# Conv features of a hybrid decoder block by seven products per tile pair, attention in a stage of its own

## The reference

```python
proj = jnp.einsum('bsd,de->bse', x, w_in[l])
q, k, v, cb, cc, ch, g_conv, g_attn = jnp.split(proj, SPLIT_POINTS, axis=-1)
# short convolution: three causal taps per channel over u = cc * ch, then times cb
y_conv = short_conv_mixer(cb, cc, ch, conv_w[l])
# blocks of 128 queries against 256 keys; ALiBi bias, mask, and a sink logit in max and denominator
y_attn = sliding_window_attention(q, k, v, attn_sinks[l])
merged = jax.nn.sigmoid(g_conv) * y_conv + jax.nn.sigmoid(g_attn) * y_attn
mix = jnp.einsum('bse,ed->bsd', merged, w_out[l])
x = layer_norm(ALPHA * x + mix, ln1_g[l], ln1_b[l])
hid = jax.nn.silu(x @ w_gate[l]) * (x @ w_up[l])
x = layer_norm(ALPHA * x + hid @ w_down[l], ln2_g[l], ln2_b[l])
```

## Time and profile before

| | before |
|---|---|
| median of three runs | 1379.73 us |
| the profiled execution's own time | 1379.17 us |
| its span, first to last instruction | 1377.3 us |
| TensorE busy | 1366.4 us, 6650 matmuls |
| VectorE busy | 779.7 us |
| ScalarE busy | 484.3 us |
| GpSimd busy | 596.9 us |
| mean granted TensorE clock | 0.999 |

### The profile page before, as it was taken

The page is one execution under the profiler, slowest core; times in us unless marked ns, Lnnn a source line. Parts: engine busy times, 40 slices in busy tenths (PEclk is TensorE's granted clock), DMA queues, the critical chain, the costliest instruction groups (busy, mean ns, idle before and its releaser), DMA issues. The chain is left out here.

```text
span 1377.3 us, 19023 instructions
## 1 busy us (share of the span) xinstructions
PE 1366.4 (99%) x6650; PEld 1200.2 (87%) x6650; DVE 779.7 (57%) x1197; ACT 484.3 (35%) x933; POOL 596.9 (43%) x375
## 2 busy tenths in 40 slices
PE   9999999999999999999999999999999999999997
PEld 8888888888888888888888888888888888888886
DVE  3127564566447653767967944645456454464547
ACT  4434333344243433335245332322323213233143
POOL 2221223212322132124885493754737547475474
PEclk9999999999999999999999999999999999999999
DMA  6211111111111111111430131112211112121113
GB/s 184 62 46 46 41 37 51 40 46 46 46 46 34 42 46 46 46 45 48 136 93 31 46 91 33 62 52 62 69 31 61 53 61 69 31 65 56 55 54 123
DMA packets 128406, 80.22 MB, mean 58 GB/s; under 512 B 8432, under 2 KB 123120, under 8 KB 128368
## 3 DMA queue, kind: packets, MB, share of 16 engines
q1 hardware_dynamic: 128368, 79.73, 19.2%
HBM read 75.53 MB, written 4.19 MB: 58 GB/s over the span
## 5 line engine op out<-in xcount | busy, mean ns | idle before, releaser
L512 POOL TENSOR_TENSOR w_lo<-raw,w_hi 128x1024 fp32r<-128x1024 f32 x54 | 128.4, 2378 | 480.0 <-ACT w_hi L663 471.0
L1448 PE MATMUL ps<-act_hi,w_hi 128*128 128x512 f32 x848 | 322.5, 380 | 0.0
L1449 PE MATMUL ps<-act_lo,w_hi 128*128 128x512 f32 x848 | 321.4, 379 | 0.0
L1450 PE MATMUL ps<-act_hi,w_lo 128*128 128x512 f32 x848 | 321.4, 379 | 0.0
L604 POOL TENSOR_TENSOR w_lo<-raw,w_hi 128x512 fp32r<-128x512 f32 x80 | 110.4, 1381 | 204.0 <-ACT w_hi L886 204.0
L1450 PEld LDWEIGHTS ps<-act_hi,w_lo 128*128 128x128 f32 x848 | 160.2, 189 | 22.8
L1449 PEld LDWEIGHTS ps<-act_lo,w_hi 128*128 128x128 f32 x848 | 160.4, 189 | 21.6
L1448 PEld LDWEIGHTS ps<-act_hi,w_hi 128*128 128x128 f32 x848 | 160.3, 189 | 21.6
L1448 PE MATMUL ps<-hid_hi,wd_hi 128*128 128x512 f32 x320 | 121.5, 380 | 0.1
L1449 PE MATMUL ps<-hid_lo,wd_hi 128*128 128x512 f32 x320 | 121.3, 379 | 0.0
L1450 PE MATMUL ps<-hid_hi,wd_lo 128*128 128x512 f32 x320 | 121.3, 379 | 0.0
(11 more groups left out here) (213 smaller groups left out, 2539.2 us busy)
## 6 DMA issues: line engine op xcount, KB each, us to landing
raw<-in_w_in SPq DMA_DIRECT2D x52, 512.0 KB, 3.8
raw<-in_w_gate SPq DMA_DIRECT2D x40, 256.0 KB, 2.9
raw<-in_w_up SPq DMA_DIRECT2D x40, 256.0 KB, 3.1
raw_d<-in_w_down SPq DMA_DIRECT2D x20, 512.0 KB, 3.2
raw<-in_w_out SPq DMA_DIRECT2D x16, 512.0 KB, 3.7
xs<-in_x SPq DMA_DIRECT2D x8, 512.0 KB, 7.2
out<-rows SPq DMA_DIRECT2D x7, 512.0 KB, 2.6
raw_first<-in_w_down SPq DMA_DIRECT2D x2, 512.0 KB, 3.5
```

Of the source, the lines that this page charges most:

```text
L512: pool.tensor_tensor(w_lo[:, slot], raw[:, slot], fp(w_hi[:, slot]), ALU.subtract).then_inc(w_lo_s, 1)
L1448: pe.matmul(bank, w_h(t), hi, start=(t == 0), stop=False)
L1449: pe.matmul(bank, w_h(t), lo, start=False, stop=False)
L1450: last = pe.matmul(bank, w_l(t), hi, start=False, stop=(t == tiles - 1))
```

## The change

The loop over heads is replaced by two stages written out in line.

- **Conv stage.** Twelve tile pairs, (cc, ch) of all eight conv tiles and (gc, cb) of the four even ones, are computed by seven products each, as in the FFN. Blocks of w_in of 256 KB are loaded to `raw`; GpSimd forms four sums or differences and seven low parts of 128x512 for each pair. The four token sums of x are kept in `x_form`, formed by VectorE, ScalarE and GpSimd in the prologue; x's second half is kept in `res` by an extra copy (`x_kept`), the sum of the parts of the first half is formed by GpSimd (`x_sum_first`). The taps of the convolution are done within `conv_pair`.
- **Attention stage.** 24 tiles stay as units of 24 matmuls: q, ga, and the odd gc and cb of each head, 12 units to four heads' queries in place of 24. Positions of all work are counted in depth steps of three matmuls, eight to a unit: block b has its scores at 12b, the turning at 12b + 14, the values at 12b + 20, and the other engines follow lists sorted by such positions. The first block stands at the end of the four units of the first q tiles. The last head's blocks 5 to 7 run into the output projection, whose first half starts before its second half's operands exist.
- **Sink.** The sink is an extra column of the score tile, so the maximum, the exponent and its sum contain it; the score is kept negated. Four small VectorE operations and one ScalarE operation of a block fall away (`SOFT` 8 to 4).
- **Out-projection.** `x_sum(1, m)` moves from the first half's loop to the second half's, one ahead of each `out_sum`; the second half's low parts (`mix_second`) go to the end of the attention.

The output computed is the same. The core of the diff:

```diff
+CONV_PAIRS = [pair for k in range(NKV) for pair in (("cc", "ch", 2 * k), ("gc", "cb", 2 * k), ("cc", "ch", 2 * k + 1))]
+HEAD_TILES = [(0, "q", 0), (0, "q", 1)]
+for _k in range(NKV):
+    HEAD_TILES += [(_k, "ga", 0), (_k, "ga", 1), (_k, "gc", 1), (_k, "cb", 1)]
+    if _k < NKV - 1:
+        HEAD_TILES += [(_k + 1, "q", 0), (_k + 1, "q", 1)]
+UNITS = [(0, 0), (0, 1), (1, 0), (1, 1)]
...
+def block_at(b, later):
+    return TURN_OF * (b // NB) + 12 * (b % NB) + later
+PE_STEPS = sorted([(block_at(b, 0), "scores", b) for b in BLOCKS] + [(block_at(b, 14), "turn", b) for b in BLOCKS]
+                  + [(block_at(b, 20), "values", b) for b in BLOCKS])
+DVE_STEPS = scheduled(
+    [(unit_end(u) + (0.2 if HEAD_TILES[UNITS[u][0]][1] == "cb" else 0.9), "unit", u) for u in range(len(UNITS))
+     if HEAD_TILES[UNITS[u][0]][1] != "ga"],
+    [(block_at(b, 1), "scores", b) for b in BLOCKS],
+    [(block_at(b, 8.2), "exp", b) for b in BLOCKS],
+    [(block_at(b, 16.2), "turn", b) for b in BLOCKS],
+    [(block_at(b, 22.2), "values", b) for b in BLOCKS],
+    [(-28 if k == 0 else TURN_OF * k - 7.5, "keys", k) for k in range(NKV)],
+    [(-27 if k == 0 else TURN_OF * k - 3.5, "bias", k) for k in range(NKV)],
...
+            for c in range(NCP):
+                for j in range(7):
+                    conv_product(c, j)
+            def scores(b):
+                k, n = b // NB, b % NB
+                if n == 0:
+                    pe.wait_ge(prep_dve, 8 * k + 2)
+                    pe.wait_ge(q_lo_s, 8 * k + (4 if k else 8))
...
+            def values(b):
+                k, n = b // NB, b % NB
+                pe.wait_ge(pt_lo_s, k * NTURN + (turned(n, 1) + 1))
...
+            act.wait_ge(c_pair, CONV_STEPS)
+            for step, n in ACT_STEPS:
...
+            def taps(h):
+                y = res[:, j, half(h)]
+                done(f"gate{h}")
+                dve.tensor_scalar(y, u_pad[:, h * HALF:(h + 1) * HALF], cw[:, j, 0:1], None,
+                                  ALU.mult).then_inc(c_pair, 1)
+                for t in (1, 2):
+                    dve.scalar_tensor_tensor(out=y, in0=u_pad[:, h * HALF + t:(h + 1) * HALF + t],
+                                             scalar=cw[:, j, t:t + 1], in1=y, op0=ALU.mult,
+                                             op1=ALU.add).then_inc(c_pair, 1)
...
-                    dve.tensor_reduce(mx[:], prob[:, :, lo:], AX_X, ALU.max).then_inc(soft_s, 1)
-                    dve.tensor_tensor(mx[:], mx[:], snkc[:], ALU.max).then_inc(soft_s, 1)
+                dve.tensor_reduce(neg_m[:], sc[:, :, lo:], AX_X, ALU.min).then_inc(soft_s, 1)
...
+            for v in range(DT, OUT_TILES):
                 if v != OUT_TILES - 2:
+                    x_sum(1, v - DT)
                     out_sum(v)
+                if v == OUT_TILES - 3:
+                    x_sum(1, DT - 2)
```

More of the change, by code:

```diff
@@ L49 @@
 PRO_TILES = 4
-TILES = [("q", 0), ("q", 1), ("ga", 0), ("ga", 1)] + [(x, j) for j in (0, 1) for x in ("cc", "ch", "gc", "cb")]
 PRO_UNITS = [(0, 0), (1, 0), (0, 1), (1, 1), (2, 0), (2, 1), (3, 0), (3, 1)]
-NT = len(TILES)
-IN_TILES = PRO_TILES + NKV * NT
-OUT_TILES = 2 * DT
-COLS = {"q": COL_Q, "ga": COL_GA, "cc": COL_CC, "ch": COL_CH, "cb": COL_CB, "gc": COL_GC}
[L60 to L74, removed]
@@ new lines, with conv_table, conv_step @@
+CONV_B = {"u2": 1, "u3": 2, "up0": 3, "gate0": 4, "hid0": 5, "up1": 6, "part1": 7, "sum1": 8, "gate1": 9, "hid1": 10}
+def conv_table(c):
+    return CONV_A if CONV_PAIRS[c][0] == "cc" else CONV_B
+def conv_step(c, name):
+    return sum(max(conv_table(b).values()) for b in range(c)) + conv_table(c)[name]
+CONV_STEPS = conv_step(NCP - 1, "taps1")
+HEAD_TILES = [(0, "q", 0), (0, "q", 1)]
[3 more added lines that the diff above has]
+        HEAD_TILES += [(_k + 1, "q", 0), (_k + 1, "q", 1)]
@@ L514, in _, with x_sum_first @@
             pool.wait_ge(w_first_s, 1)
-            for t in range(6):
-                low_part(t + 1, t % 2)
+            def x_sum_first(m):
+                if m == 0:
+                    pool.wait_ge(x_lo_s, 8)
+                pool.tensor_tensor(res[:, m, half(0)], fp(act_hi[:, m, half(0)]), fp(act_lo[:, m, half(0)]),
+                                   ALU.add).then_inc(x_sum0, 1)
+            low_part(1, 0)
+            for m in (0, 4):
+                x_sum_first(m)
+            low_part(2, 1)
@@ L978, in _, with keep_values @@
                                   fp(act_hi[dst]), ALU.subtract).then_inc(x_lo_s, 1)
-            for i in range(4):
+            def keep_values(i):
                 j, h = PRO_UNITS[i]
@@ L989, in mixer_low @@
+            for c in range(NCP):
+                conv_pair(c)
+            dve.wait_ge(c_pair, CONV_STEPS)
             def mixer_low(h, m):
@@ new lines, in turn_probs @@
+            def turn_probs(b):
+                k, n = b // NB, b % NB
+                pe.wait_ge(soft_s, SOFT * b + SOFT)
+                if b:
+                    pe.wait_ge(pt_lo_s, k * NTURN + turned(n, 1 if n == 0 else 0))
+                for kb in range(1 if n == 0 else 0, 2):
+                    for g in range(G):
+                        last = pe.transpose(ps[:, TURN + kb, blk(g)], prob[:, g, blk(kb)], ident[:])
+                    last.then_inc(turn_s, 1)
+            def values(b):
+                k, n = b // NB, b % NB
+                pe.wait_ge(pt_lo_s, k * NTURN + (turned(n, 1) + 1))
+                if n == 0:
+                    pe.wait_ge(prep_dve, 8 * k + 8)
+                if b:
+                    pe.wait_ge(o_s, 3 * (b - 1) + 2)
+                kbs = [1] if n == 0 else [0, 1]
+                for kb in kbs:
+                    for part in (pt_hi, pt_lo):
+                        last = pe.matmul(ps[:, OUT, :], vs[:, n - 1 + kb, :], folded(part[:, kb]),
+                                         start=(kb == kbs[0] and part is pt_hi),
+                                         stop=(kb == 1 and part is pt_lo))
+                last.then_inc(values_s, 1)
```

946 lines of the change are left out of this document (613 added, 333 removed).

## The result

The changed kernel takes 1387.95 us in the median (1386.09 to 1390.26, 4 runs) against 1379.65 (1379.35 to 1380.01, 4 runs) for the kernel before: a ratio of 1.0061, with a 95% interval of 1.0041 to 1.008. It is slower by 0.6%, clear of the noise. The forecast was 1372.0 and the range ended at 1386.

What follows compares the result with a forecast made beforehand. TensorE was taken as the bound, busy 1366.4 of 1377.3 us. 31.1 us saved against 23.8 us of new waits gave 1379.2 - 7.3 = 1371.9, rounded to 1372 us; range 1357 to 1386.

Steps and rivals of the forecast that it cites:

- What is removed: Twelve tile pairs: 144 fewer matmuls at 0.216 us each on TensorE, saving 31.1 us.
- the floor: Time with the full saving and no new TensorE waits: 1379.2 - 31.1 = 1348.1 us.
- Prologue and conv stage: Kernel start and conv products: new TensorE waits of 0.3 us (bounds 0 and 4) and 1 us in all.
- port rival: Conv stage: GpSimd and VectorE sharing the port exceed TensorE's time, 10.4 us in all, 1382 us; chance 0.13.
- Handover and first scores: Wait before the first q unit, 4.9 us; block 0's wait for the q low parts, 2.9 us.
- Interior blocks: Attention blocks not at a head's end: VectorE's work fits on average, 0.5 us of waits for all.
- rival of late low parts in every block: Attention: each of 28 interior blocks late by 0.7 us, costing 19 us, time 1391; chance 0.13.
- Head ends: Last block of a head, before its values: low parts late, 2 us at each of three, 6 in all (bounds 0 and 12).
- The last block: Output projection, first half: last block's low parts late behind mix_second and x_sum, 3.2 us (bounds 0 and 6).
- `mean(1)`: Output projection, second half: three more x_sums delay mean(1) in full, 4.5 us taken (2.1 to 6.5).
- The clock: Low granted clock at the gap before the first q unit: 0.5 us added for the way back (bounds 0 and 3).
- 0.15 on slower: Whole kernel: chance 0.15 that the time comes out over 1382.5 us.

Runs made afterwards that it cites:

- last-block experiment: Changed kernel with the six late mixer low parts moved behind the last block's low part on VectorE: 1385.67 us, 1.0042 of the kernel before.
- experiment on the sums of the second half: Changed kernel with five second-half x_sums moved after the first half and three ahead of out_sum(9): 1382.83 us, 1.0032 of the kernel before.
- all waits taken up: Changed kernel with five reorderings together (first weight parts, head ends, mixer low parts, second-half sums, first scores): 1357.64 us, 0.9845 of the kernel before.
- what was left: The all waits taken up kernel with four mixer low parts behind out_sum(5), last head's mixer steps a block later, second mean two steps later: 1356.01 us.

## Why the prediction failed, step by step

**What is removed: right.** The own time 1386.09 less 29.7 of gaps and 8.5 of clock is 1347.9; the floor was put at 1348.1.

**Prologue and conv stage: right, but for a term that comes and goes.** In the profile of the changed kernel neither has a new gap (0 against 1.3 taken). In three of the ten profiles of kernels with the conv stage there is one of 1.98 us near 85, always at the fourth product of the second pair (`THIRD_DIFF`), waiting for VectorE's first sum `u2`. VectorE of the last-block experiment there:

```profile
80.20 1.68 DVE L1372 TENSOR_TENSOR u_pad<-cu_st,cu 128x512 f32<-128x512 f32 x1
81.92 1.39 DVE L1326 TENSOR_SCALAR res<-u_pad,cw 128x512 f32<-128x512 f32 x1
```

The product into u_pad took 1.68 us and the first tap 1.39, where the changed kernel's profile has 0.92 and 0.49. In the one GpSimd's low parts began at 80.06, just ahead of the product, in the other at 79.37, behind it (78.26 to 79.18). So who comes first decides on 1.7 us of VectorE's time here. These kernels' first units also start up to 1.2 us apart. The port rival was thus wrong in the size (10 us) and right in the place. GpSimd is not full in the conv stage of the changed kernel (fifth of the busy times), and TensorE idles only behind its end:

```profile
78.00:277.00 199.00, 197.89 (x917) 172.90 (x915) 114.35 (x140) 55.98 (x93) 154.51 (x116) 1.00 0.21 59
```

**Handover and first scores: right.** 4.9 taken, 4.95 measured; 2.9 taken, 2.99 measured. Both chains were walked in full from rows 3 to 6, with nothing beside them. **Interior blocks: right** (0.5 taken, none measured but the 0.67 at 641, put down to issue), and so the rival of late low parts in every block was wrong.

**Head ends: right in place and cause, 1.8 us short.** Three of 2.6 us against three of 2. The walk had the low parts at 18.0 us from the scores of the head's last block (376.8 at the first end); there they ended at 396.55, 19.8 us on. Most of the difference is one operation, the gating (L1470): 2.00 us beside a GpSimd weight part of 2.37, where 0.43 is its time alone. The prediction had named this collision and allowed 1.5 us for it.

**The last block: mechanism right, size under half.** Taken at 3.2 us (bounds 0 and 6), measured 7.01. TensorE, VectorE and GpSimd in the changed kernel:

```profile
650.62 1.89 PE L1791 MATMUL ps<-m_hi,w_lo 128*128 128x512 f32 x8
659.35 0.77 PE L1957 MATMUL ps<-pt_hi,vs 128*128 128x512 f32 x1 [6.84 <-DVE pt_lo L1456]
659.91 0.63 PE L1957 MATMUL ps<-pt_lo,vs 128*128 128x512 f32 x1
```

```profile
648.01 3.48 DVE L1381 SCALAR_TENSOR_TENSOR m_lo<-res,m_hi 128x512 fp32r<-128x512 f32 x2
651.40 0.68 DVE L1475 TENSOR_TENSOR res<-act_hi,act_lo 128x512 f32<-128x512 f32 x1
652.19 0.69 DVE L1524 SCALAR_TENSOR_TENSOR res<-res,ps 128x512 f32<-128x512 f32 x1
652.79 5.10 DVE L1381 SCALAR_TENSOR_TENSOR m_lo<-res,m_hi 128x512 fp32r<-128x512 f32 x3
657.81 1.27 DVE L1456 TENSOR_TENSOR pt_lo<-ps,pt_hi 128x512 fp32r<-128x512 f32 x2
```

```profile
647.69 2.64 POOL L739 TENSOR_TENSOR w_lo<-raw,w_hi 128x1024 fp32r<-128x1024 f32 x1 [1.98 <-ACT w_hi L1056]
652.95 1.65 POOL L728 TENSOR_TENSOR acc<-acc,res 128x512 f32<-128x512 f32 x1 [2.62 <-DVE res L1524]
654.56 2.79 POOL L739 TENSOR_TENSOR w_lo<-raw,w_hi 128x1024 fp32r<-128x1024 f32 x1
```

The queue is the one that was walked, five low parts, one x_sum and one out_sum ahead of `pt_lo`. But two low parts took 3.48 us and three took 5.10, where 0.68 is the time of one alone. Taken singly they are 2.87 and 0.68, then 0.68, 1.75 and 2.82: each long one ends 0.5 us behind the GpSimd operation beside it. The last two stood against 1.65 + 2.79 us of GpSimd. At their own spacing (0.6 us; 0.8 for the x_sum) the seven operations from 648.01 would have ended 4.4 us later, and `pt_lo` at 653.7, for a gap of some 1.6 us (an estimate: 7.0 less the 5.4 us by which it was later, at 659.08). The sum had held operations in it, but by too little, and the bound of 6 was no bound.

**`spread(0)`: missed.** The x_sum ahead of `out_sum(11)` (2.08 us behind GpSimd) holds up the reciprocal that TensorE waits for: 1.29 us. Only `mean(1)` was looked at for late x_sums.

**`mean(1)`: right in place, cause and size** (4.5 taken, 4.98 measured). The stretch that answers to the earlier trace rows:

```profile
718.36 2.84 DVE L1475 TENSOR_TENSOR res<-act_hi,act_lo 128x512 f32<-128x512 f32 x1
...
721.91 0.68 DVE L1475 TENSOR_TENSOR res<-act_hi,act_lo 128x512 f32<-128x512 f32 x1
...
729.43 0.68 DVE L1475 TENSOR_TENSOR res<-act_hi,act_lo 128x512 f32<-128x512 f32 x1
730.23 0.69 DVE L1524 SCALAR_TENSOR_TENSOR res<-res,ps 128x512 f32<-128x512 f32 x1
```

```profile
730.99 1.26 POOL L728 TENSOR_TENSOR acc<-acc,res 128x512 f32<-128x512 f32 x1 [4.23 <-DVE res L1524]
```

```profile
727.20 0.38 PE L1802 MATMUL ps<-act_hi,w_lo_b 128*128 128x512 f32 x1
732.40 2.04 PE L1989 MATMUL ps<-acc,mean_of 128*128 128x512 f32 x2 [4.82 <-POOL acc L728]
```

Two of the three x_sums cost 0.68 us and one 2.84; the out_sum is at 730.23 instead of 726.24, and TensorE is ready at 727.4.

**The clock: the step that failed.** It was taken at 0.5 us with bounds 0 and 3, for one gap, the handover. It cost 8.5 us in the profiled execution, at four gaps. The tail of the earlier trace rows had been read as if some 5 us of idle time were needed, from a place where TensorE does no more work. The way back, which no row showed, was put at 0.5. Behind the handover alone it cost 1.7. The other gaps of the forecast, five of them, got no clock term at all. Of the miss of 16 us (14 against the profiled execution), 8.0 are this, 3.8 the last block, 1.8 the head ends, 1.3 the spread, 0.7 the gap at 641 and 0.6 small differences at the mean, the handover and the scores; prologue, conv stage, interior blocks and the floor gave back 2.0. With the clock as it was taken, the profiled execution would stand at 1378, inside the range, but still level with the kernel before: so the range failed by the clock, and the gain that was forecast by the clock and the last block together. The Trainium skill (TensorE: Matmul & The Clock Gate, "What's actually happening") has the clock at half speed by default and released by activity. The low stretches after gaps agree with it; the prediction cited the sentence and did not use it on its own list of gaps.

The chances were off by the same step: 0.15 on slower, for a mechanism that did not come.

## What to carry to other kernels

On an engine that is 99% busy, list the new gaps, and then put a second price on every gap of 2 us and more: here a fall of the granted clock, 78.5 us over 49 gaps of 2.3 to 7.1 us in the profiles, 1.6 us each in the mean, with ten of them that cost nothing. Saved work on the bound engine is only as good as the order of the others: with the same 144 matmuls less, one order lost 8 us and another won 23. And in a stretch where GpSimd works without a pause, count each VectorE operation with two SBUF inputs as one that stands behind a GpSimd operation (here up to 2.9 us in place of 0.68), all of them, before you call a queue hidden.

## What the runs showed of the hardware that was not expected

**A gap of 2.3 to 3 us brought the lower clock in 17 cases of 27.** Over the twelve profiles, by the length of the gap:

```
gap of TensorE, us    gaps   clock at 0.50 behind them
1.0 to 2.1              33    1
2.3 to 3.0              27   17
4.5 to 7.1              22   22
```

The one fall in the first row came behind 1.24 us followed by the variance's sixteen one-column matmuls. Equal gaps of the same trace differ: at 397 the clock fell, at 484 and 569 it did not. A low stretch lasted 3.4 us in most cases, 6.8 in others and 10.2 once (behind 7.08 us), and cost 1.4 to 3.3 us of TensorE's time. The changed kernel's runs differ by 4 us, and their granted clock goes with it (0.988 to 0.991); those of the kernel before, which has no such gap, lie within 1.3.

**GpSimd and VectorE alternate, whole instruction by whole instruction.** The five x_sums in a row of the experiment on the sums of the second half, and GpSimd beside them:

```profile
679.19 8.52 DVE L1475 TENSOR_TENSOR res<-act_hi,act_lo 128x512 f32<-128x512 f32 x5
```

```profile
679.78 2.93 POOL L739 TENSOR_TENSOR w_lo<-raw,w_hi 128x1024 fp32r<-128x1024 f32 x1 [1.11 <-ACT w_hi L1056]
682.67 1.73 POOL L728 TENSOR_TENSOR acc<-acc,res 128x512 f32<-128x512 f32 x1
684.36 2.81 POOL L739 TENSOR_TENSOR wd_lo<-raw,wd_hi 128x1024 fp32r<-128x1024 f32 x1
```

Taken singly the five are 0.68, 0.69, 2.87, 1.76 and 2.85 us: three GpSimd operations, three long sums, each ending 0.5 us behind its own. GpSimd pays as well: its operations behind one of VectorE's are 2.8 and 1.7 us long, where 2.4 and 1.3 are their times alone. Four mixer low parts took 6.86 us with two GpSimd operations beside them (all waits taken up), and six took 5.97 with one (last block) and 10.51 with four (what was left). So the price of a queue follows the GpSimd operations that fall into it, one for one; the 1.7 us for each VectorE operation that the first two of these stretches give are only a mean. The Trainium skill (SBUF — State Buffer, "Who interferes with whom") says that such a pair excludes each other for the instruction; the traces agree.

Left open: why of two equal gaps one brings the lower clock, and why the gap of 0.67 us at 641, which the profile puts down to issue, appears.
